# A two-block model forward pass: another order in the state-space stage, and two more expert slabs fetched during routing

## The reference

```python
def ssd_chunked(x, dt, A, Bm, Cm):   # per chunk of tokens, per head
    cs = jnp.cumsum(dt * A, axis=2)
    Lmat = jnp.exp(where(incl, cs_i - cs_j, -inf))
    y_intra = (Cm Bm^T * Lmat) @ (x * dt)
    chunk_states = Bm^T @ (x * dt * exp(cs_last - cs))
    # scan over chunks
    y_inter = (Cm @ h) * exp(cs)
    h = h * exp(cs_last) + chunk_states
```

## Time and profile before

| | us |
|---|---|
| median of 3 runs (lowest, highest) | 3774.42 (3770.18, 3776.53) |
| the profiled execution | 3775.39 |
| its span, first to last instruction | 3773.6 |
| TensorE matmuls busy | 3358.8 (89%) |
| VectorE, ScalarE, GpSimd busy | 1713.0, 1074.6, 307.5 |
| `ssd` stage, from its first instruction to the next stage's | 745.6 to 972.2 |
| `route` and `pick` stages, from SP's first issue | 1083.8 to 1176.4 |
| `experts` stage, to its last matmul's end | 1176.4 to 1408.9 |

### The profile page before, as it was taken

The page is one execution under the profiler, slowest core; times in us unless marked ns, Lnnn a source line. Parts: engine busy times, 40 slices in busy tenths (PEclk is TensorE's granted clock), DMA queues, the critical chain, the costliest instruction groups (busy, mean ns, idle before and its releaser), DMA issues. The chain is left out here.

```text
span 3773.6 us, 39304 instructions
## 1 busy us (share of the span) xinstructions
PE 3358.8 (89%) x15418; PEld 2425.6 (64%) x15418; DVE 1713.0 (45%) x2459; ACT 1074.6 (28%) x1529; POOL 307.5 (8%) x260
## 2 busy tenths in 40 slices
PE   4999999888859776999998889998999998889997
PEld 3475764634645224888784568887888784568886
DVE  2557667556441004442326744433443326644433
ACT  2232231223321004222213643222322213543222
POOL 1222020011010001000002000000000002000001
PEclk6999999999969997999999999999999998999998
DMA  2101010000225981222211022222222211022221
GB/s 77 57 34 46 1 46 34 23 34 1 90 79 214 420 368 57 98 91 100 105 46 46 1 89 100 100 96 78 96 99 100 100 37 59 1 83 104 92 100 56
DMA packets 50693, 326.33 MB, mean 86 GB/s; under 512 B 7040, under 2 KB 7424, under 8 KB 13056
## 3 DMA queue, kind: packets, MB, share of 16 engines
q1 hardware_dynamic: 50560, 324.52, 23.0%
HBM read 321.35 MB, written 2.10 MB: 86 GB/s over the span
## 5 line engine op out<-in xcount | busy, mean ns | idle before, releaser
L364 PE MATMUL psum<-ffn_x_hi,ffn_w_hi 128*128 128x512 f32 x1408 | 548.1, 389 | 2.6 <-DVE ffn_x_lo L320 2.5
L364 PE MATMUL psum<-ffn_x_hi,ffn_w_lo 128*128 128x512 f32 x1408 | 547.8, 389 | 0.0
L364 PE MATMUL psum<-ffn_x_lo,ffn_w_hi 128*128 128x512 f32 x1408 | 547.7, 389 | 0.0
L309 DVE TENSOR_TENSOR ffn_w_lo<-ffn_raw,ffn_w_hi 128x2048 fp32r<-128x2048 f32 x128 | 293.4, 2292 | 423.3 <-ACT ffn_w_hi L280 423.3
L280 ACT ACTIVATE ffn_w_hi<-ffn_raw 128x2048 fp32r<-128x2048 f32 x128 | 245.3, 1916 | 566.9 <-PE psum L364 566.9
L104 PE MATMUL psum<-mix_normed,mix_ring 128*128 128x512 f32 x832 | 367.6, 603 | 21.4 <-DMA mix_ring<-w_gdn 8.4
L364 PEld LDWEIGHTS psum<-ffn_x_hi,ffn_w_hi 128*128 128x128 f32 x1408 | 264.3, 188 | 61.9 <-DVE ffn_w_lo L316 7.3
L104 PEld LDWEIGHTS psum<-mix_normed,mix_ring 128*128 128x128 f32 x832 | 160.2, 193 | 223.8 <-issue 214.6
L364 PEld LDWEIGHTS psum<-ffn_x_hi,ffn_w_lo 128*128 128x128 f32 x1408 | 264.3, 188 | 55.2
L364 PEld LDWEIGHTS psum<-ffn_x_lo,ffn_w_hi 128*128 128x128 f32 x1408 | 264.3, 188 | 54.6
L364 PE MATMUL psum<-ffn_hid_hi,ffn_w_hi 128*128 (+1 forms) x704 | 273.9, 389 | 0.0
(11 more groups left out here) (474 smaller groups left out, 5435.9 us busy)
## 6 DMA issues: line engine op xcount, KB each, us to landing
ffn_raw<-w_ffn SPq DMA_DIRECT2D x128, 1024.0 KB, 4.8
mix_ring<-w_experts SPq DMA_DIRECT2D x48, 1024.0 KB, 13.6
mix_ring<-w_mix SPq DMA_DIRECT2D x32, 1024.0 KB, 7.2
mix_normed<-w_experts SPq DMA_DIRECT2D x24, 1024.0 KB, 13.6
experts_slabs<-w_experts SPq DMA_DIRECT2D x24, 1024.0 KB, 13.6
mix_ring<-w_gdn SPq DMA_DIRECT2D x16, 1024.0 KB, 4.9
mix_ring<-w_ssd SPq DMA_DIRECT2D x10, 1024.0 KB, 4.8
mix_ring<-w_out SPq DMA_DIRECT2D x7, 1024.0 KB, 7.2
```

The costliest lines, as they stand in the source:

```text
L309: dve.tensor_tensor(w_lo[:, q, :], raw[:, q, :], w_hi[:, q, :].bitcast(F32), ALU.subtract)\
L364: ins = pe.matmul(out, wp[:, q, w], xp, start=start and a == 0, stop=stop and a == 2)
```

## The change

In the `ssd` stage the lists of TensorE, ScalarE and VectorE for group 0 get another order; no operation is added or removed. TensorE does decays 0 to 7 before `tiles(2)`, and `tiles(3)` and `tiles(4)` move behind `outputs(0, 1)` and `outputs(0, 2)`. ScalarE does exponentials 0 to 11 in one go, then Silus 0 to 3, exponentials 12 to 15, Silus 4, 5, 8 and 9. VectorE does `out(0, 1)` before `conv(4)`.

In the expert part the ring gets two more slots, so that eight slabs are fetched ahead: slabs 0 to 5 in `route`, 6 and 7 in `pick`. One new slot is a buffer of its own (`experts_ahead`), the other is the place of the position tables. These are now read again in the `scatter` stage, not in `route`. To make room, the masks and scalars of the recurrences move into a context of their own, `recurrence_memory`, which ends before the output projection.

The delta-rule stage, where ScalarE and GpSimd do the convolution of v, is the same in both kernels.

```diff
--- before.py
+++ after.py
@@ -27,6 +27,7 @@
 NT = T // P
 SLAB = 2048
 SLOTS = 4
+AHEAD = 2
 EPS = 1e-6
 
 GH = 8
@@ -1377,12 +1378,19 @@
             tiles(1)
             for n in range(4):
                 decay(0, n)
-            for j in range(1, 5):
-                for n in range(4 * j, 4 * j + 4) if j < 4 else ():
-                    decay(0, n)
-                if j < 4:
-                    tiles(j + 1)
-                outputs(0, j - 1)
+            for n in range(4, 8):
+                decay(0, n)
+            tiles(2)
+            outputs(0, 0)
+            for n in range(8, 12):
+                decay(0, n)
+            outputs(0, 1)
+            tiles(3)
+            for n in range(12, 16):
+                decay(0, n)
+            outputs(0, 2)
+            tiles(4)
+            outputs(0, 3)
             decay(1, 0)
             decay(1, 1)
             tokens(1)
@@ -1432,16 +1440,13 @@
                 act.activation(rstd, rstd, ACT.Sqrt).then_inc(rooted, 1)
 
             copy_b(0)
-            for n in (6, 7, 0, 1):
+            for n in (6, 7):
                 silu(n)
-            exps(0, range(0, 8))
-            for n in (2, 3):
-                silu(n)
-            exps(0, range(8, 12))
-            for n in (4, 5):
+            exps(0, range(0, 12))
+            for n in (0, 1, 2, 3):
                 silu(n)
             exps(0, range(12, 16))
-            for n in (8, 9):
+            for n in (4, 5, 8, 9):
                 silu(n)
             exps(1, range(0, 2))
             copy_b(1)
@@ -1536,8 +1541,8 @@
             conv(2)
             out(0, 0)
             scores(0, range(8, 12))
+            out(0, 1)
             conv(4)
-            out(0, 1)
             scores(0, range(12, 16))
             out(0, 2)
             out(0, 3)
@@ -1575,7 +1580,8 @@
     weight = cut(small, 6 * T, NE // 2)
     xs = cut(m.moe_xs, 0, KD, NE * CAP)
     spare = m.xT[:, :, :].rearrange("p k t -> p (k t)")
-    ring = [m.ring[:, s, :] for s in range(SLOTS)] + [spare[:, s * SLAB:(s + 1) * SLAB] for s in range(2)]
+    ring = [m.ring[:, s, :] for s in range(SLOTS)] + [m.moe_ahead[:, :], m.rope_tables[:, 0:SLAB]]
+    ring += [spare[:, s * SLAB:(s + 1) * SLAB] for s in range(2)]
     n_early = len(ring)
 
     def fetch(sp, n):
@@ -1584,15 +1590,13 @@
     by_expert = lambda a: a.unsqueeze(2).to_broadcast([P, NT, NE])
 
     with stage(nc, m, "route") as (block, sem):
-        loaded, logits, exped, shifted, normed, turned, placed, back, chain, tables = sem(10)
+        loaded, logits, exped, shifted, normed, turned, placed, back, chain = sem(9)
 
         @block.sync
         def _(sp):
             sp.dma_start(router, io["w_router"]).then_inc(loaded, 16)
-            sp.dma_start(m.rope_tables, io["const_f"][:, m.rope_at:m.rope_at + m.rope_width]).then_inc(tables, 16)
-            for n in range(SLOTS):
+            for n in range(SLOTS + AHEAD):
                 fetch(sp, n)
-            sp.wait_ge(tables, 16)
 
         @block.tensor
         def _(pe):
@@ -1647,7 +1651,7 @@
         @block.sync
         def _(sp):
             sp.wait_ge(turned, 8)
-            for n in (4, 5):
+            for n in range(SLOTS + AHEAD, n_early):
                 fetch(sp, n)
 
         @block.vector
@@ -1848,8 +1852,13 @@
     y_hi, y_lo = (parts.enter_context(nc.sbuf_tensor(f"experts_y_{n}", [P, 2, NE // 2, P], F32R))[:, :, :, :]
                   for n in ("hi", "lo"))
     with stage(nc, m, "scatter") as (block, sem):
-        hi_done, split, done, renewed, squared, folded = sem(6)
+        hi_done, split, done, renewed, squared, folded, tables = sem(7)
         sq = cut(m.norm_tmp, 0, 2, T)
+
+        @block.sync
+        def _(sp):
+            sp.dma_start(m.rope_tables, io["const_f"][:, m.rope_at:m.rope_at + m.rope_width]).then_inc(tables, 16)
+            sp.wait_ge(tables, 16)
 
         @block.scalar
         def _(act):
@@ -2843,7 +2852,7 @@
         return ctx.enter_context(nc.sbuf_tensor(name + "_sb", [P, *shape], dt))
 
     m.signals = [ctx.enter_context(nc.semaphore(f"signal_{i}")) for i in range(48)]
-    m.early = [ctx.enter_context(nc.semaphore(f"expert_slab_{i}")) for i in range(SLOTS + 2)]
+    m.early = [ctx.enter_context(nc.semaphore(f"expert_slab_{i}")) for i in range(SLOTS + AHEAD + 2)]
     m.ps = ctx.enter_context(nc.psum_tensor("psum", [P, 8, T], F32))
     m.resid = sb("resid", KD, T)
     m.squares = sb("squares", T)[:, :]
@@ -2880,7 +2889,7 @@
 
 
 @contextmanager
-def mixer_memory(nc, m, name, first=False):
+def mixer_memory(nc, m, name):
 
     with ExitStack() as ctx:
         def sb(what, *shape, dt=F32):
@@ -2890,20 +2899,6 @@
         m.ring_flat = sb("ring", SLOTS * SLAB)
         m.ring = m.ring_flat[:, :].rearrange("p (s n) -> p s n", s=SLOTS)
         m.norm_tmp = sb("norm_tmp", 2 * T)
-        if first:
-            m.cols = sb("group_cols", 64)[:, :]
-            m.masks = sb("masks", 14 * P, dt=U8)
-            by_level = m.masks[:, :].rearrange("p (l s n) -> p l s n", s=2, n=P)
-            m.lower, m.upper = by_level[:, :, 0, :], by_level[:, :, 1, :]
-            m.scal_buf = sb("scalars", 4 * 192 + 192 + 2 * 64 + 128)
-            m.scal, at = {}, 0
-            for n, heads in (("g", NG), ("step", NG), ("from_start", NG), ("to_end", NG), ("total", NG),
-                             ("beta", GH), ("beta_decay", GH), ("step_to_end", SH)):
-                m.scal[n] = cut(m.scal_buf, at, NT, 2, heads)
-                at += NT * 2 * heads
-            m.cur_buf = sb("group_scalars", 4 * NT * 2 * 8)
-            m.cur = {n: cut(m.cur_buf, i * NT * 2 * 2, NT, 2, 2)
-                     for i, n in enumerate(("beta", "beta_decay", "to_end", "total", "g"))}
         yield
 
 
@@ -2912,7 +2907,31 @@
 
     with nc.sbuf_tensor("experts_put", [P, NE // 2 * T], F32R) as m.moe_put, \
             nc.sbuf_tensor("experts_xs", [P, KD * NE * CAP], F32) as m.moe_xs, \
+            nc.sbuf_tensor("experts_ahead", [P, SLAB], F32) as m.moe_ahead, \
             nc.sbuf_tensor("experts_small", [P, 6 * T + NE // 2], F32) as m.moe_small:
+        yield
+
+
+@contextmanager
+def recurrence_memory(nc, m):
+
+    with ExitStack() as ctx:
+        def sb(what, *shape, dt=F32):
+            return ctx.enter_context(nc.sbuf_tensor(f"mix1_{what}", [P, *shape], dt))
+
+        m.cols = sb("group_cols", 64)[:, :]
+        m.masks = sb("masks", 14 * P, dt=U8)
+        by_level = m.masks[:, :].rearrange("p (l s n) -> p l s n", s=2, n=P)
+        m.lower, m.upper = by_level[:, :, 0, :], by_level[:, :, 1, :]
+        m.scal_buf = sb("scalars", 4 * 192 + 192 + 2 * 64 + 128)
+        m.scal, at = {}, 0
+        for n, heads in (("g", NG), ("step", NG), ("from_start", NG), ("to_end", NG), ("total", NG),
+                         ("beta", GH), ("beta_decay", GH), ("step_to_end", SH)):
+            m.scal[n] = cut(m.scal_buf, at, NT, 2, heads)
+            at += NT * 2 * heads
+        m.cur_buf = sb("group_scalars", 4 * NT * 2 * 8)
+        m.cur = {n: cut(m.cur_buf, i * NT * 2 * 2, NT, 2, 2)
+                 for i, n in enumerate(("beta", "beta_decay", "to_end", "total", "g"))}
         yield
 
 
@@ -3134,9 +3153,9 @@
 def program(nc, io):
     with ExitStack() as ctx:
         m = memory(nc, ctx)
-        with mixer_memory(nc, m, "mix1", True):
+        with mixer_memory(nc, m, "mix1"):
             with nc.sbuf_tensor("mix1_mixed", [P, 2 * KD, T], F32) as m.mixed:
-                with work_memory(nc, m, "recurrences"):
+                with recurrence_memory(nc, m), work_memory(nc, m, "recurrences"):
                     start_stage(nc, m, io)
                     resid_norm_stage(nc, m, "norm1", m.gains["norm1"], m.xT)
                     scalars_stage(nc, m, io)
```

## The result

The changed kernel takes 3751.66 us, median of 4 runs (3747.5 to 3753.31), against 3774.1 (3770.18 to 3776.53): ratio 0.9937, 95% interval 0.9924 to 0.9949, 22.4 us less. Forecast were 3739.0 and a range of 3732 to 3750: the direction is right, the size is off by 12.7 us, and the time lies outside the range. The profiled execution took 3750.3 us, 25.1 less than the one of before.

A forecast was written before the change was run, and what follows sets the result against it. TensorE, busy 89% of the span, bounds most of the kernel; the slab stream bounds the experts stage. Profiled 3775.39 - 30.4 (state-space block) - 5.0 (slabs) = 3740.0, or 3739.0 us against the median; range 3732 to 3750.

The forecast's parts named there:

- TensorE's work, 82.3 us: State-space block, group 0: TensorE's own work 82.3 us of 113.07, the other 30.8 gaps and half-clock work.
- the end of the three waits: State-space stage: TensorE's three waits for ScalarE's exponentials, 23.0 us in all, go; group 1 starts 30.4 us sooner.
- decay steps 0 to 7: State-space group 0: needing only ScalarE's exponentials and GpSimd's layouts, they run without waits, 1.75 us each.
- the unknown that costs most: State-space group 0: VectorE's scores 0 to 7 before conv(2) take 14.4 us, no loss; upper bound loses 1.8 us.
- The rule quoted there: State-space scores: two-SBUF-input VectorE and SBUF-reading GpSimd operations exclude each other per instruction; loss 0 to 1.8 us.
- The slabs, 5.0 us: Experts stage: 88 slabs streamed instead of 90, so the stream and last product end 5.0 us sooner.
- The tables' read, zero: Scatter stage: reading the position tables there, 1152 KB, costs zero; 5.8 us if it stood bare.
- the table load without a drain: ScalarE, decays 12 to 15: exp table load of 1.28 us without drain, TensorE waits 0.35 us; with drain 1.7.
- 35.4 worked out: Whole kernel: the gain from the state-space block, 30.4 us, and from the slabs, 5.0 us, together.
- the wait comes back: Rival, 5%: at decay 12 TensorE waits 6.9 us for ScalarE behind late conv(2), plus 2.2 of half clock: 3748.1.

The follow-up runs named there:

- the one with the decays split: Changed kernel, but TensorE does decays 6 and 7 behind tiles(2) and VectorE scores 6 and 7 behind conv(2): 3741.17 us, ratio 0.9909.
- the slabs alone: Changed kernel with the old ssd_groups, so only the two slots, moved table read and memory contexts: 3768.33 us, ratio 0.9994.
- the four layouts: Changed kernel, but GpSimd lays group 0's decay inputs into four buffers in turn instead of two: 3741.78 us, ratio 0.9916.

## Why the prediction was wrong

- *TensorE's work, 82.3 us, and the end of the three waits.* Right: blocks of 82.45 to 82.7 us in the kernels in which TensorE did not wait for a layout, 83.3 in the one with the decays split.
- *The step that failed:* "decay steps 0 to 7 need only these and GpSimd's layouts (1.39 us with contention, against a step of 1.75), so they run 784.4 to 798.4". The layout of decay 6 took 8.18 us. It cost 6.60 us of wait and 1.98 of half clock, 8.6 of the 12.7 us that the forecast missed. In "the unknown that costs most" I bounded the same meeting from VectorE's side alone: how slow can the products get, 0 to 1.8 us. The products lost nothing (0.68 us each); the layout did. An exclusion has two possible losers, and the one that TensorE waits for next is the dear one.
- *The rule quoted there.* The Trainium skill (SBUF — State Buffer, section "SBUF: two separate sides") has whoever starts first keep the port pair that VectorE and GpSimd share for a whole instruction. The traces agree that two SBUF inputs are what collides (a layout beside products with a PSUM input takes its 1.05 us). They disagree on the length: VectorE kept GpSimd out for 12 to 16 instructions, until it paused. They also disagree on who wins: a layout that started 0.07 us ahead of the first product was shut out.
- *The trace of before had it.* The group 1 part of the same stage, which I took as unchanged, shows a layout in a dense run of products, then TensorE's wait for it, and VectorE's side (rows of the kernel before, GpSimd, TensorE, VectorE):

```profile
947.45 4.06 POOL L1287 TENSOR_TENSOR mix_norm_tmp<-const_sb,mix_scalars 128x512 f32<-128x512 f32 x2 [3.67 <-PE psum L1341]
```

```profile
950.11 1.12 PE L1339 MATMUL psum<-mix_norm_tmp,const_sb 128*128 128x512 f32 x2 [1.02 <-POOL mix_norm_tmp L1287]
```

```profile
947.26 0.68 DVE L1509 TENSOR_TENSOR mix_ring<-mix_ring,recurrences_work 128x512 f32<-128x512 f32 x1
...
949.07 0.73 DVE L1515 SCALAR_TENSOR_TENSOR recurrences_work<-recurrences_work,mix_group_scalars,psum 128x512 f32<-128x512 f32 x1
```

  The two layouts of the first row took 4.06 us; the longest of the line's 32 is 2.6 us and their median 1.06. TensorE had the layout 1.04 us after VectorE's run of products gave way at 949.07 to an operation that reads PSUM. A look at the longest of a group, beside its median, would have pointed at an upper bound: a layout may last as long as VectorE's run. With 12 products that is, as an estimate, 7.2 + 1.05 = 8.3 us where a step lasts 1.75: 6.5 us of wait and 2 of half clock, a case at 3747.5 with a chance of its own, and a range to some 3756.
- *The slabs, 5.0 us.* Right: 5.3, 6.2 and 4.2 us in the profiles of the changed kernel, the slabs alone and the four layouts, with an unchanged stream.
- *The tables' read, zero, and the table load without a drain.* Right: the load of 850.90 lasts 1.28 us, and the exponential starts at 852.19.
- *The rest, 12.7 - 8.6 = 4.1 us:* no step of the sum stands against it. Where TensorE did not wait for a layout the medians are 30.0 and 31.9 us under the kernel before, with 35.4 worked out; that sum is a ratio of 0.9906, inside the intervals of both (0.9903 to 0.9929, 0.9895 to 0.9923), and their profiled spans are 36.9 and 34.2 us shorter. Single profiles of the untouched second block take between 2292.4 and 2306.4 us. What is left of the miss can't be told from this scatter, and its cause stays open.
- *Rivals.* None had this mechanism. The second ("the wait comes back") priced a loss of 9.1 us, near the 8.6, but by ScalarE behind a late convolution, which did not happen: that its size fits is luck.

## What to carry to other kernels

When VectorE multiplies two SBUF tiles many times without a pause, a GpSimd operation that comes then (here one with two SBUF inputs) can last as long as the whole run. Before packing work closer, ask for every GpSimd result that is on the path: how long is the VectorE run that it may meet, and read the longest of its instructions, not the median. Four remedies took TensorE's wait away here: let GpSimd run further ahead (more buffers), put TensorE work that does not need the result in front of the work that does, read one operand from PSUM, or let VectorE wait between products (tried with a wait before each but the first).

## What the runs showed of the hardware

VectorE's products with two SBUF inputs kept a GpSimd product (two SBUF inputs as well) out for 7.1 to 9.5 us, over 12 to 16 instructions, although GpSimd had come within 0.5 us of the run's start. So it was in all ten traces in which such a run of group 0 met a layout at its start with no pause in it and no product that had waited. Where a product had waited for GpSimd just before, the next GpSimd instruction got in after at most one product (1.39 us in place of 1.05), and VectorE then paid 0.85 us each time. A pause of 0.11 us between products lets GpSimd in too, at 0.67 us for VectorE. That the waiting product makes the difference was forecast for two runs and held in both.

It is not the whole rule. In group 1 the same meeting stands in all sixteen traces: an operation of VectorE waits 0.08 us for a layout (943.56 in the kernel before), and the next layout comes 0.19 us into the sixth product behind it. In twelve traces, the kernel before among them (the row at 947.45 above), it is shut out until the run ends, 2.60 us. In four it gets in at 1.39 us; the changed kernel is one of them, and for that reason has no wait of TensorE there:

```profile
927.60 1.40 POOL L1288 TENSOR_TENSOR mix_norm_tmp<-const_sb,mix_scalars 128x512 f32<-128x512 f32 x1 [3.67 <-PE psum L1342]
```

The distances agree within 0.01 us in all sixteen. So some products after a wait either outcome is possible; what makes VectorE keep GpSimd out or let it in was not found.
